# Second half of the chunked scan: three scalings from VectorE to ScalarE, and two buffers for y

## The reference, cut to what matters

```
def step(state, inp):                                # per chunk
    y_diag = einsum('blsgr,bsgrp->blgrp', cb[..., None] * decay, xc)
    y_off = einsum('blgn,bgrpn->blgrp', cc, state) * exp(acum)[..., None]
    new_state = (state * exp(acum[:, -1])[..., None, None]
                 + einsum('blgn,blgr,blgrp->bgrpn', bc, to_end, xc))
    return new_state, y_diag + y_off
...
y = y + xh * d_skip.reshape(SSD_N_GROUPS, SSD_HEADS_PER_GROUP)[..., None]
...
act = gelu(einsum('td,thkd->thk', xb, u))            # u = expert_u[eidx]
return einsum('thk,thkd->td', g * act, v)            # v = expert_v[eidx]
```

## Time and profile before

| | us |
|---|---|
| three runs, median (lowest to highest) | 2750.47 (2743.41 to 2753.17) |
| the profiled execution, its own time | 2750.07 |
| its span in the profile | 2748.2 |
| the second half's scan in it, first DVE instruction L1049 to the last of L1100 | 888.87 to 1061.2 |
| busy in the span: PE, DVE, ACT, POOL | 2328.0, 1756.2, 576.9, 1102.6 |

### The profile page before, as it was taken

How to read it: one execution, slowest core, us unless ns; L and a number is a source line. 1 busy time by engine, 2 the same in 40 slices (tenths; PEclk the granted TensorE clock), 3 DMA queues, 4 the chain that set the end, 5 groups by cost and what they waited for, 6 DMA issues and landing times. The chain is left out here.

```text
span 2748.2 us, 28360 instructions
## 1 busy us (share of the span) xinstructions
PE 2328.0 (85%) x9768; PEld 1645.1 (60%) x9768; DVE 1756.2 (64%) x3623; ACT 576.9 (21%) x1562; POOL 1102.6 (40%) x1058
## 2 busy tenths in 40 slices
PE   7998999997882897999788795497569799999988
PEld 6856888683662555878455473245466455547665
DVE  3315510159999998686788887978876777731510
ACT  4421300021332222000111201340223210112321
POOL 0000000002655777454555575677564677700000
PEclk9998999998996998999899897698787899999999
DMA  4322234336999999999997899999998899963386
GB/s 159 137 108 93 76 154 153 107 131 275 386 414 401 364 399 390 417 414 416 415 374 263 331 413 411 390 366 413 364 415 343 355 414 414 414 247 111 134 301 227
DMA packets 187054, 832.08 MB, mean 303 GB/s; under 512 B 22416, under 2 KB 22672, under 8 KB 174112
## 3 DMA queue, kind: packets, MB, share of 16 engines
q0 software_dynamic: 147456, 536.94, 49.9%
q1 hardware_dynamic: 39456, 293.33, 27.1%
HBM read 828.09 MB, written 2.10 MB: 302 GB/s over the span
## 5 line engine op out<-in xcount | busy, mean ns | idle before, releaser
L1256 POOL DMA_INDIRECT expert_rows<-in_peer_u,chosen x512 | 529.9, 1035 | 1040.9 <-DVE chosen L1859 640.5
L1256 POOL DMA_INDIRECT expert_rows<-in_peer_v,chosen x512 | 569.3, 1112 | 260.9 <-issue 126.6
L1347 DVE SCALAR_TENSOR_TENSOR expert_rows<-expert_rows,expert_sum 128x1024 f32<-128x1024 f32 x384 | 451.8, 1217 | 77.2 <-DMA expert_rows<-in_peer_u,chosen 72.4
L1357 DVE SCALAR_TENSOR_TENSOR h<-expert_rows,expert_coef,h 128x1024 f32<-128x1024 f32 x194 | 249.8, 1288 | 41.5 <-DMA expert_rows<-in_peer_v,chosen 36.6
L1357 DVE SCALAR_TENSOR_TENSOR u<-expert_rows,expert_coef,u 128x1024 f32<-128x1024 f32 x190 | 244.8, 1288 | 33.9 <-DMA expert_rows<-in_peer_v,chosen 31.3
L1296 PE MATMUL expert_sum<-expert_rows,expert_diag 128*128 128x512 f32 x496 | 235.1, 619 | 23.5 <-ACT expert_diag L1283 17.7
L2997 PE MATMUL mlp_up<-mlp_xT,mlp_slab 128*128 128x384 f32 (+1 forms) x1024 | 226.7, 383 | 1.2 <-ACTq L132 0.7
L2989 PE MATMUL mlp_down<-mlp_slab,upT 128*128 128x512 f32 x512 | 222.2, 592 | 0.0
L2997 PEld LDWEIGHTS mlp_up<-mlp_xT,mlp_slab 128*128 128x128 f32 x1024 | 157.3, 194 | 73.6 <-issue 5.7
L1296 PEld LDWEIGHTS expert_sum<-expert_rows,expert_diag 128*128 128x128 f32 x496 | 92.0, 195 | 127.2 <-issue 119.2
L1347 DVE SCALAR_TENSOR_TENSOR expert_rows<-expert_rows,u 128x1024 f32<-128x1024 f32 x128 | 151.7, 1225 | 24.0 <-DMA expert_rows<-in_peer_u,chosen 17.3
(11 more groups left out here) (562 smaller groups left out, 3639.2 us busy)
## 6 DMA issues: line engine op xcount, KB each, us to landing
expert_rows<-in_w_in SPq DMA_DIRECT2D x27, 2048.0 KB, 7.4
in_slab<-in_w_in SPq DMA_DIRECT2D x22, 2048.0 KB, 10.7
mlp_slab<-in_w_up SPq DMA_DIRECT2D x64, 512.0 KB, 6.7
mlp_slab<-in_w_down SPq DMA_DIRECT2D x64, 512.0 KB, 6.7
mix_slab<-in_w_in SPq DMA_DIRECT2D x10, 2048.0 KB, 10.9
out_slab<-in_w_out SPq DMA_DIRECT2D x6, 2048.0 KB, 10.1
expert_rows<-in_ssd_w_out SPq DMA_DIRECT2D x4, 2048.0 KB, 8.0
expert_rows<-in_peer_w_q SPq DMA_DIRECT2D x4, 2048.0 KB, 9.8
```

Of the source, the lines that this page charges most:

```text
L1256: pool.indirect_dma_start(out=self.row(n), out_offset=None, in_=self.tables[0 if dot else 1], in_offset=bass.IndirectOffsetOnAxis(ap=picks ...
L1347: dve.scalar_tensor_tensor(self.row(n), self.row(n), 1.0, u, ALU.mult, ALU.mult, accum_out=dot).then_inc(self.rows_used, 1)
L1357: dve.scalar_tensor_tensor(o, self.row(n), coef, o, ALU.mult, ALU.add).then_inc(self.rows_used, 1)
```

## The change

In the second half's scan alone (`if bg`):

- ACT, in round q after the four Exp, runs `scale_group(q)`: x of the group by the skip weight, the state of the group by its decay, and the carried part of y by from_start straight from PSUM into y. Each is four instructions of 64 columns, one for each head, with the head's factor as the scale. Twelve instructions a round, 192 in the scan.
- DVE loses L1051, L1084 and L1066 there: four of 128x1024 and 32 of 128x256. It waits for three new semaphores in place: `state_scaled` before the addition to the state, `carried_in_y` and `x_scaled` before the additions to y.
- `staged` is given after xend and no more after the scaled x.
- y has two buffers; ACT may write the carried part of group q when group q - 2 is finished (y_ready).
- PE waits for `carried_in_y` before the inner part of the same group, since both are in one PSUM bank.

The first half's scan keeps its instructions and their order.

```diff
-        y = sbuf(ctx, "y", [P, GW])
+        y = [sbuf(ctx, f"y{i}", [P, GW]) for i in range(2 if bg else 1)]
...
+            def scaled_by_head(dst, src, scale):
+
+                for h in range(HPG):
+                    cols = slice(h * HDIM, (h + 1) * HDIM)
+                    ins = act.activation(dst[:, cols], src[:, cols], ACT.Copy, scale=scale[:, h:h + 1])
+                return ins
+
+            def scale_group(q):
+
+                c, g = q // GROUPS, q % GROUPS
+                h, w = slice(g * HPG, (g + 1) * HPG), slice(g * GW, (g + 1) * GW)
+                act.wait_ge(staged, q // QUAD + 1)
+                scaled_by_head(xs[:, c, w], xs[:, c, w], rows[:, 2, h]).then_inc(x_scaled, 1)
+                act.wait_ge(off_done, FIRST + q + 1)
+                scaled_by_head(state[:, w], state[:, w], whole[:, c, h]).then_inc(state_scaled, 1)
+                if q >= 2:
+                    act.wait_ge(y_ready, q - 1)
+                scaled_by_head(y[q % 2][:], yo[q % 2][:, 1, :], from_start[:, c, h]).then_inc(carried, 1)
...
+                    if bg:
+                        scale_group(q)
                 if q >= 2:
                     square_group(q - 2)
...
-                chain.mark(dve.tensor_tensor(e, d, per_head(to_end[:, c, h], HDIM), ALU.mult))
-                dve.tensor_tensor(x, x, per_head(rows[:, 2, h], HDIM), ALU.mult).then_inc(staged, 1)
+                ins = dve.tensor_tensor(e, d, per_head(to_end[:, c, h], HDIM), ALU.mult)
+                if not bg:
+                    chain.mark(ins)
+                    ins = dve.tensor_tensor(x, x, per_head(rows[:, 2, h], HDIM), ALU.mult)
+                ins.then_inc(staged, 1)
...
-                ychain.link(dve.tensor_tensor(heads(y[:], HDIM), heads(yo[q % 2][:, 1, :], HDIM),
-                                              per_head(from_start[:, c, h], HDIM), ALU.mult))
-                ychain.link(dve.tensor_tensor(y[:], y[:], yo[q % 2][:, 0, :], ALU.add))
-                ychain.link(dve.tensor_tensor(y[:], y[:], xs[:, c, w], ALU.add))
+                own = y[q % len(y)][:]
+                if bg:
+                    dve.wait_ge(carried, q + 1)
+                    dve.wait_ge(x_scaled, q + 1)
+                else:
+                    ychain.link(dve.tensor_tensor(heads(own, HDIM), heads(yo[q % 2][:, 1, :], HDIM),
+                                                  per_head(from_start[:, c, h], HDIM), ALU.mult))
+                ychain.link(dve.tensor_tensor(own, own, yo[q % 2][:, 0, :], ALU.add))
+                ychain.link(dve.tensor_tensor(own, own, xs[:, c, w], ALU.add))
...
+                    if bg:
+                        dve.wait_ge(state_scaled, q + 1)
+                    else:
+                        ychain.link(dve.tensor_tensor(heads(state[:, w], HDIM), heads(state[:, w], HDIM),
+                                                      per_head(whole[:, c, h], HDIM), ALU.mult))
...
             def inside(q):
                 pe.wait_ge(mixer_ready, q + 1)
+                if bg:
+                    pe.wait_ge(carried, q + 1)
```

More of the change, by code:

```diff
@@ L965, in scan @@
         meta_ready = sem("meta_ready")
+        x_scaled, carried, state_scaled = sem("x_scaled"), sem("carried_in_y"), sem("state_scaled")
         if half:
@@ L1065, in finish_group @@
                 h, w = slice(g * HPG, (g + 1) * HPG), slice(g * GW, (g + 1) * GW)
-                ychain.link(dve.tensor_tensor(heads(y[:], HDIM), heads(yo[q % 2][:, 1, :], HDIM),
-                                              per_head(from_start[:, c, h], HDIM), ALU.mult))
-                ychain.link(dve.tensor_tensor(y[:], y[:], yo[q % 2][:, 0, :], ALU.add))
-                ychain.link(dve.tensor_tensor(y[:], y[:], xs[:, c, w], ALU.add))
+                own = y[q % len(y)][:]
[7 more added lines that the diff above has]
+                ychain.link(dve.tensor_tensor(own, own, xs[:, c, w], ALU.add))
                 o = z[:, c, w]
-                dve.tensor_tensor(o, o, y[:], ALU.mult).then_inc(y_ready, 1)
+                dve.tensor_tensor(o, o, own, ALU.mult).then_inc(y_ready, 1)
             for q in range(N + 1):
@@ L1083, in _ @@
                     dve.wait_ge(off_done, FIRST + q + 1)
-                    ychain.link(dve.tensor_tensor(heads(state[:, w], HDIM), heads(state[:, w], HDIM),
-                                                  per_head(whole[:, c, h], HDIM), ALU.mult))
+                    if bg:
[3 more added lines that the diff above has]
+                                                      per_head(whole[:, c, h], HDIM), ALU.mult))
                     dve.tensor_tensor(state[:, w], state[:, w], grown[q % 2],
```

## The result

The changed kernel took 2764.3 us (median of 20 runs, 2757.16 to 2769.18 but for one of 7121.77 that the ratio leaves out) beside 2753.78 us for the kernel before (20 runs, 2743.21 to 2762.3) on the same chip: ratio 1.0033, 95% interval 1.0023 to 1.0043. That is slower, by about 9 us, where no change was forecast and the range ended at 2754. The profiled execution took 2764.45 us, with a span of 2762.6 (before: 2750.07 and 2748.2).

A forecast was written before the change was run, and what follows sets the result against it. The prediction took POOL's stream of gathers to bound the scan. Start -1.1 and end -1.2 us, all else 0, made -2.3 us from 2750.1: 2748 us, called the same, range 2741 to 2754.

The forecast's parts named there:

- The bound: Second half's scan: POOL's gathers, 1.322 us each, are the slower stream; neither DVE nor the ring of 16 buffers sets their pace.
- DVE's saving: Scan: DVE loses 18.8 us of work, nearly all turning into waits for gathered rows, which it meets near 950.
- Worth on the path: nothing in the middle of the stage: Middle of the scan: DVE's shorter round, 8.6 us from 9.8, gains nothing on the path.
- Rival A: Scan: fewer short DVE instructions hold up POOL, gathers quicken to 1.26 us each, 6.6 us gained, total 2741; chance 0.12.
- The start, -1.1 us: Scan's start: `staged` comes one L1051 earlier, so PE starts and the whole stream of gathers moves 1.1 us earlier.
- The end, -1.2 us: After unit 252: DVE's last round and finish lose short instructions, gaining 1.2 us (bounds 0 and -1.3).
- ACT: Scan: ACT's twelve new instructions take 3.1 us a round, hidden behind DVE's five expert units; cost 0.
- PE's wait: Before the inner part of group q, PE waits for `carried_in_y`, written a full round earlier; cost 0.
- downstream: Merge after the scan: it starts earlier by what the scan gives, so the gain carries through whole.
- Rival C: Scan: PE's clock drops as it waits for DVE's mixer, and its buffers hold up POOL; 19 us slower, 2767; chance 0.05.
- B: Scan: DVE is the bound after all and its 18.8 us come through, 2731; chance 0.04.
- D: Later stages: the few us are lost again, waiting for something that did not move, 2750; chance 0.15.

The follow-up runs named there:

- after: The changed kernel with the whole change, all three scalings on ACT, against the kernel before: 2764.3 us, ratio 1.0033.
- x_and_state: Against the kernel before, only the scalings of x and of the state go to ACT, y's stays on DVE: 2744.51 us, ratio 0.9965.
- pad2: The changed kernel with two useless DVE instructions of 128x256 added in each round: 2756.36 us, ratio to the kernel before 1.0004.
- x_only: Against the kernel before, only the skip scaling of x goes to ACT: 2750.07 us, ratio 0.9987.
- after_again: The changed kernel as it is, run again on the same chip as two of the padded kernels: 2765.57 us, ratio to the kernel before 1.0047.
- pad1: The changed kernel with one useless DVE instruction of 128x256 added in each round: 2748.11 us, ratio to the kernel before 0.9977.
- pad3: The changed kernel with three useless DVE instructions of 128x256 added in each round: 2757.36 us, ratio to the kernel before 1.0009.
- act_extra: The kernel before with twelve more ACT instructions a round, written to a spare tile, DVE and PE as before: 2751.86 us, ratio 0.9986.
- y_only: Against the kernel before, only the scaling of the carried part of y goes to ACT: 2752.64 us, ratio 0.9995.
- one_input_after: The changed kernel, with DVE's expert instructions for units 128 to 255 reading one SBUF input, not adding: 2747.28 us, ratio to the kernel before 0.9983.
- state_only: Against the kernel before, only the state's scaling goes to ACT: 2748.01 us, ratio 0.9979.

## Why the prediction was wrong

*The bound.* Right: POOL's stream of gathers is the slower one, and DVE's time is no bound. 111 gathers, landings and the ring behaved as read.

*DVE's saving.* Right in size (18.8 us by the rows, 17.1 in the busy sum), and right that DVE would turn it into waits. The waits came to 28.6 us more, not some 18, and from 929 on instead of 950.

***"Worth on the path: nothing in the middle of the stage"*: this is the step that failed.** It took POOL's 1.322 us as a constant of the gathers. It was a sum, 1.24 us plus stretches that DVE's order of work sets, and the change moved them: 1.444 us, +13.4 us over 110 intervals. The rows for it were at hand: the 1.35 us of the earlier trace rows, always at the same place of a round. Laid beside DVE's rows they would have given the fixed end 2.09 us after the first expert instruction, and from this the remainder of a shorter round: 8.23 - 6 x 1.24 = 0.8. That gives the sign and about half of the loss; the other half, behind the waits, these rows don't give.

*Rival A* named the right mechanism, DVE holding up POOL, and gave it the wrong sign. It reasoned that fewer short instructions hold up POOL less. That is so, but they are worth little: beside them POOL lost 0.03 to 0.18 us at a time, 1.1 us in the whole stage before and nothing in "after", while the long ones that follow them cost up to 1.0 each, by phase. No case of mine let POOL's own instructions become longer. The Trainium skill, "SBUF — State Buffer", Who interferes with whom, says that the engine which issues first has the shared ports for its whole instruction and that the other blocks fully; the constant 2.09 us agrees, being one DVE instruction (1.15) and one whole POOL instruction (0.94). A gather reads its row numbers (`chosen`) from SBUF, so that rule covers it. I leant instead on the page's remark, inferred there, that such an instruction leaves the writing of descriptors alone; these gathers are held all the same, and no run shows at which of their steps.

*The start, -1.1 us.* The step is right where PE's clock is: from the first L1049 to the first gather it is 6.86 us before and 5.72 in x_and_state, pad2, x_only and after_again, 1.14 less where 1.13 was forecast. In the profiled "after" PE's first products ran at the lower of the clock's two levels (granted clock 0.50 from 892 to 894, where it was 1.00 before):

```profile
892.27 1.19 PE L1206 MATMUL yo<-state,choice 128*128 128x256 f32 x2 [1.05 <-DVE xend L1072]
893.25 1.06 PE L1208 MATMUL sums<-xend,h 128*128 128x256 f32 x2
```

1.19 us, against 0.67 in the earlier trace rows, and the gain was gone (7.28). It comes and goes from one execution to the next: pad1, pad3, act_extra, y_only and one_input_after show 1.19 too.

*The end, -1.2 us.* Only 0.5 of it is seen (15.1 us from the last gather to the scaling of z, 15.5 before), since the last rows came late: DVE waited 2.28 and 2.55 us for two of the last five.

*ACT.* Four of the new instructions take 0.90 to 1.07 us, and the three quartets, which overlap a little, 2.83 from the first start to the last end, where 3.1 was taken:

```profile
933.81 1.07 ACT L1003 ACTIVATE choice<-choice,head_rows 128x64 f32<-128x64 f32 x4
934.77 1.06 ACT L1003 ACTIVATE state<-state,whole 128x64 f32<-128x64 f32 x4
935.72 0.92 ACT L1003 ACTIVATE y<-yo,from_start 128x64 f32<-128x64 f32 x4
```

Hidden, but for the first two rounds, in which DVE waited 2.7 us for the scaled state (a sign of being wrong that the prediction had named; 2.4 in round 0, where the five expert rows of a round before aren't there as cover). act_extra shows that the work itself is free.

*PE's wait, the second y, downstream.* As said: PE doesn't appear among those that wait for `carried_in_y`, and the merge carried the delay through whole.

*Rival C*, slower by PE's clock, had the sign and, at 2767, nearly the size, but by luck, for the reason is wrong: POOL waited for PE's buffers 13.4 us instead of 13.0, and act_extra has the same clock without the loss. B and D didn't occur.

## What to carry to other kernels

When an engine's instruction has two durations in a trace (here 0.94 and 1.35 us), lay it beside the neighbour's in time order before you call its rate a constant: the rate that bounds the kernel may be set by the order of an engine that is not on the path. Where two engines with near-equal beats share something, what remains of the loop's length after whole beats decides the loss, so less work can cost more, and a kernel with one part of the change (here x and state on ACT, y left on DVE) may beat both the whole and nothing; time the parts one by one and in pairs. A saving on an engine that will only wait is no safe zero, since its waits change when it starts.

## What was not expected of the hardware

- An indirect DMA's instruction on POOL (0.935 us) that starts 0.10 to 1.13 us into a SCALAR_TENSOR_TENSOR of 128x1024 with two SBUF inputs ends 2.08 to 2.11 us after that one's start: 208 gathers in eleven traces, without an exception. Beside the form with a single SBUF input it isn't held (100 gathers, at most 0.95 us).
- A TENSOR_TENSOR of 128x1024 holds it as well, and the gather then ends 2.02 to 2.04 us after its start (56 gathers); one of 128x256 holds it only with two SBUF inputs. In the kernel before, POOL's gather beside L1051, which started at 906.12:

```profile
906.16 1.99 POOL L1256 DMA_INDIRECT expert_rows<-in_peer_v,chosen  x1 [0.30 <-issue]
```

- Starts up to 0.08 us after the expert instruction's cost nothing (411 gathers), though 0.04 us did beside L1051. What decides between them there stays open.
- The some 6 us by which state_only and pad1 beat the kernel before are more than their scans show (0 and 0.6 us). One profile each doesn't settle where the rest comes from; from the start of z's scaling to the end of the span the thirteen traces differ among themselves, from 1684.9 to 1693.3 us. The same goes for pad3, whose scan is 8.8 us longer and whose median is 3.4 us higher.
